# Four units per chunk instead of three and one, and both first weight blocks split before the chunk loop

## The reference

```python
def _ffn_sublayer(h, mod, g_pre, g_post, w_in, w_out):
    shift, scale, gate = mod
    u = _modulate(_rmsnorm(h, g_pre), shift, scale)      # rmsnorm, then * (1 + scale) + shift
    a, b = jnp.split(u @ w_in, 2, axis=-1)
    y = (jax.nn.silu(a) * b) @ w_out
    return h + MACARON_W * gate * _rmsnorm(y, g_post)
```

## Time and profile before

| what | us |
|---|---|
| median of three timed runs | 2501.28 |
| span of the profiled execution | 2505.6 |
| TensorE matmul busy | 2363.2 (94%) |
| VectorE busy | 1239.4 (49%) |
| ScalarE busy | 1023.2 (41%) |
| the two-part products (L914 to L916), share of the chain that ended last | 66% |

### The profile page before, as it was taken

One profiled execution on the slowest core, in us unless ns is written; L12 is line 12 of the kernel. 1 busy time (PEld: TensorE's weight loads), 2 busy tenths in 40 slices (PEclk: granted clock), 3 DMA queues, 4 the chain that ended last, 5 costly groups with the idle time before them and its releaser, 6 DMA issues.

```text
span 2505.6 us, 41414 instructions
## 1 busy us (share of the span) xinstructions
PE 2363.2 (94%) x15342; PEld 2029.3 (81%) x15342; DVE 1239.4 (49%) x1709; ACT 1023.2 (41%) x1459; POOL 33.5 (1%) x35
## 2 busy tenths in 40 slices
PE   5999999999898999998999999899799989998998
PEld 5888888777677888887888878777699979988997
DVE  4332335755656322337332336655564576856665
ACT  4332224543455332235322224543564455344443
POOL 0000000000000000000000000000000000000000
PEclk8999999899998999998999999999899988999899
DMA  9553552322214544532323543421256543214221
GB/s 303 185 176 94 172 177 86 118 85 85 85 35 135 157 141 138 173 124 72 110 79 113 186 140 96 105 89 58 68 148 172 153 143 96 68 61 135 79 68 51
DMA packets 396899, 298.16 MB, mean 119 GB/s; under 512 B 10846, under 2 KB 358756, under 8 KB 396644
## 3 DMA queue, kind: packets, MB, share of 16 engines
q1 hardware_dynamic: 363274, 231.12, 31.3%
q10 hardware_dynamic: 33498, 65.35, 7.4%
HBM read 295.38 MB, written 1.06 MB: 118 GB/s over the span
## 4 chain that ended last, share of the span: by engine, by line
PE 80%; DVE 9%; ACT 4%; issue 3%; DMA 2%; SPq 1%; DVEq 0%; POOL 0%; ACTq 0%; POOLq 0%
PE banks L914 22%; PE banks L915 22%; PE banks L916 22%; PE banks L1172 3%; DVE wl L2095 3%; PE banks L819 2%; ACT wh L1601 2%; PE banks L855 1%; SPq L670 1%; DVE wl L2113 1%; PE banks L1023 1%; ACT uR L1592 1%; DMA scratch<-in_ada_w 1%; PE banks L1044 1%; ACT yT L1593 1%
## 5 line engine op out<-in xcount | busy, mean ns | idle before, releaser
L914 PE MATMUL banks<-uR,wh 128*128 128x512 f32 (+2 forms) x2368 | 837.2, 354 | 41.7 <-DVE uR L2080 25.7
L915 PE MATMUL banks<-uR,wh 128*128 128x512 f32 (+2 forms) x2368 | 822.9, 348 | 0.0
L916 PE MATMUL banks<-uR,wl 128*128 128x512 f32 (+2 forms) x2368 | 821.6, 347 | 0.0
L2095 DVE TENSOR_TENSOR wl<-wraw,wh 128x2048 fp32r<-128x2048 f32 (+2 forms) x214 | 453.1, 2117 | 426.2 <-ACTq L1541 421.4
L1601 ACT ACTIVATE wh<-wraw 128x2048 fp32r<-128x2048 f32 (+2 forms) x224 | 398.7, 1780 | 478.6 <-PE banks L916 448.9
L914 PEld LDWEIGHTS banks<-uR,wh 128*128 128x128 f32 (+1 forms) x2368 | 460.6, 194 | 105.2 <-issue 41.1
L916 PEld LDWEIGHTS banks<-uR,wl 128*128 128x128 f32 (+1 forms) x2368 | 459.9, 194 | 52.9
L915 PEld LDWEIGHTS banks<-uR,wh 128*128 128x128 f32 (+1 forms) x2368 | 460.7, 195 | 49.9 <-issue 0.5
L914 PE MATMUL banks<-gR,wh 128*128 128x512 f32 (+1 forms) x704 | 256.3, 364 | 4.2 <-DVEq L2001 4.1
L915 PE MATMUL banks<-gR,wh 128*128 128x512 f32 (+1 forms) x704 | 255.2, 363 | 0.0
L916 PE MATMUL banks<-gR,wl 128*128 128x512 f32 (+1 forms) x704 | 255.2, 362 | 0.0
(11 more groups left out here) (305 smaller groups left out, 2419.9 us busy)
## 6 DMA issues: line engine op xcount, KB each, us to landing
wraw<-in_ffn_w_in SPq DMA_DIRECT2D x176, 512.0 KB, 5.1
ada_buf<-in_ada_w ACTq DMA_DIRECT2D x27, 2048.0 KB, 8.4
wraw<-in_w_in SPq DMA_DIRECT2D x56, 512.0 KB, 4.6
wraw<-in_ffn_w_out SPq DMA_DIRECT2D x64, 384.0 KB, 4.0
wraw<-in_ffn_w_out SPq DMA_DIRECT2D x64, 320.0 KB, 3.7
wraw<-in_da_w_in SPq DMA_DIRECT2D x24, 512.0 KB, 4.6
wraw<-in_na_w_in SPq DMA_DIRECT2D x24, 512.0 KB, 4.5
yT<-in_ada_w ACTq DMA_DIRECT2D x4, 2048.0 KB, 8.6
```

What stands on the lines that cost most here:

```text
L914: mm(o, a[0], b[0], start=first, stop=False)
L915: mm(o, a[0], b[1], start=False, stop=False)
L916: return mm(o, a[1], b[0], start=False, stop=last)
L2095: do(V.tensor_tensor(wl[:, s, 0:n], wraw[:, s, 0:n], wh[:, s, 0:n].bitcast(F32), ALU.subtract), w_lo)
```

## The change

It does three things at the start of each of the six stages.

1. `together` gets four units: both units of B0 and both of B1. It takes 12 matmuls per chunk, not 9, and no unit runs alone behind the loop. The number of matmuls is the same. The fourth unit needs a fourth bank: in da and na bank 7 instead of 5 (`FIRST_BANKS`), in the FFN stages the fourth of the `gemm` banks.
2. B1 is split whole before the chunk loop. `w_half` is gone; PE waits for `w_lo` of B0 and of B1 before its first matmul of the stage. The splits are in halves by rows of the slot, no longer by columns.
3. In `residual` all halves come one place earlier. Behind an FFN stage the first half of B0 now stands before the first variance, the second behind it, the first half of B1 before the reading of the third sums (L2172 in the kernel before), and its second half behind the second variance. Behind da and na, B0 has been split by then, and the halves of B1 stand behind the first and the second variance.

In ffn00 and ffn01 the transposition of the adaLN row (`ada_turn`, L829) on PE now comes behind the fourth unit. ScalarE's and SyncE's instructions and their order are the same.

```diff
+        FIRST_BANKS = (2, 3, 6, 7)
...
-                    ins = [product_step(o, both(ws[j // 2], k, slice(j % 2 * P, j % 2 * P + P)), (rhs2 if j == 2 and rhs2 else rhs)(k),
+                    ins = [product_step(o, both(ws[j // 2], k, slice(j % 2 * P, j % 2 * P + P)), (rhs2 if j >= 2 and rhs2 else rhs)(k),
...
             def first_weights():
-
-                w = weights(0, DC, 256)
-                pe.wait_ge(w_half, tl["half"].up())
-                return [w, [x[:, 1, 0:DC * 256].rearrange("p (k n) -> p k n", k=DC) for x in (wh, wl)]]
+                return [weights(s, DC, 256) for s in range(2)]
...
-                os = [ga("unit", n) for n in range(-8, -5)]
+                os = [ga("unit", n) for n in range(-8, -4)]
...
-                w = weights(1, DC, 256)
...
-                                for ins in together([gbank()[:, 0:T - c0] for a in range(3)], ws, lambda k: both(u2, k, slice(c0, T)),
+                                for ins in together([gbank()[:, 0:T - c0] for a in range(4)], ws, lambda k: both(u2, k, slice(c0, T)),
                                                     [u0 + len(streams) * (k + 1) for k in range(DC)]):
                                     ins.then_inc(gemm_full, 1)
+                            if first:
                                 continue
                             w = weights(s, DC, 2 * P)
-                            for a in range(1 if first else 0, 2):
+                            for a in range(2):
...
+                b = tl["split"].n
                 early, x, root = stat[:, 0, 8:8 + 3 * nt], stat[:, 0, 20:20 + nt], stat[:, 1, 0:nt]
                 o, free = product(small)
                 do(V.tensor_scalar(early[:, 0:nt], o[:, 0:nt], 1.0 / D, EPS, ALU.mult, ALU.add))
                 do(V.tensor_copy(early[:, nt:3 * nt], o[:, nt:3 * nt]), free)
+                if st.startswith("ffn"):
+                    rest_part(b, 0)
                 o, free = product(small)
                 do(stt(stat[:, 0, 0:nt], o[:, 0:nt], 1.0 / D, early[:, 0:nt], ALU.mult, ALU.add), free, var_ready)
-                b = tl["split"].n
                 if st.startswith("ffn"):
-                    rest_part(b, 0, False)
+                    rest_part(b, 1)
                     b += 1
+                else:
+                    rest_part(b, 0)
                 dve.wait_ge(root_ready, tl["root"].up())
                 two_parts(0, nt)
                 if st.startswith("ffn"):
-                    rest_part(b - 1, 1, False, w_lo)
+                    rest_part(b, 0)
...
-                if to in SUB:
-                    rest_part(b, 0, True, w_half)
-                else:
-                    rest_part(b, 0, False)
-                if to not in SUB or to == "na":
-                    rest_part(b, 1, to in SUB, w_lo)
+                rest_part(b, 1)
...
-                if to in SUB and to != "na":
-                    rest_part(b, 1, True, w_lo)
```

More of the change, by code:

```diff
@@ L328, in build @@
         gy_ready = sem("gy_ready")
-        w_half = sem("w_half")
         gm_ready = sem("gm_ready")
@@ L593, in take @@
                 uses[bank] += 1
-            for n in range(-8, -5):
-                take(("unit", n), 6 if n == -6 else n + 10)
+            for n in range(-8, -4):
+                take(("unit", n), FIRST_BANKS[n + 8])
             for n in DA_STEPS:
                 g, i = da_unit(n)
-                if i is not None and n >= -5:
-                    take(("unit", n), n + 10 if n < -4 else None)
+                if i is not None and n >= -4:
+                    take(("unit", n))
                 if da_rot(n) is not None:
@@ L621, in na_products @@
             for m in range(-8, 24):
-                bank = 6 if m == -6 else m + 10 if m < -4 else turn % 2
+                bank = FIRST_BANKS[m + 8] if m < -4 else turn % 2
                 turn += m >= -4
@@ L806, in _ @@
             tl = {k: Tally() for k in ("u", "g", "w", "sq", "sum", "diag", "qkv", "v", "probn", "probT", "bias", "on",
-                                       "vh", "aa", "ada", "adat", "p", "sq2", "half")}
+                                       "vh", "aa", "ada", "adat", "p", "sq2")}
             mm = nc.tensor.matmul
@@ L985, in da_heads @@
                     if i is not None:
-                        if n >= -5 and i in (0, 2, 4):
+                        if n >= -4 and i in (0, 2, 4):
                             w = weights((3 * g + i // 2) % 2, DC, 256)
-                        if n >= -5:
+                        if n >= -4:
                             o = ga("unit", n)
@@ L1080, in na_heads @@
                 ws = first_weights()
-                os = [unit_bank(m) for m in (-8, -7, -6)]
-                for ins in together([*os[0:2], os[2][:, 0:SEQ]], ws, lambda k: both(u2, k),
+                os = [unit_bank(m) for m in range(-8, -4)]
+                for ins in together([*os[0:2], *[o[:, 0:SEQ] for o in os[2:4]]], ws, lambda k: both(u2, k),
                                     [u0 + 2 * (k + 1) for k in range(DC)], lambda k: both(u2, k, slice(CTX, T))):
                     ins.then_inc(ga_full, 1)
-                w = weights(1, DC, 256)
                 for m in NA_STEPS:
@@ L1089, in na_heads @@
                     n, j = divmod(m, 2)
-                    if i is not None and m >= -5:
+                    if i is not None and m >= -4:
                         if i in (0, 2, 4):
@@ L2100, in rest_next, with rest_part @@
                     rest(b % 2, SIZES[b])
-            def rest_part(b, j, by_columns, *signals):
+            def rest_part(b, j):
                 if b < len(SIZES):
@@ L2109, in half_of @@
                     def half_of(x):
-                        x = x[:, b % 2, 0:2 * n]
-                        return x.rearrange("p (k n) -> p k n", k=DC)[:, :, j * P:j * P + P] if by_columns else x[:, j * n:j * n + n]
-                    do(V.tensor_tensor(half_of(wl), half_of(wraw), half_of(wh).bitcast(F32), ALU.subtract), *signals)
+                        return x[:, b % 2, j * n:j * n + n]
+                    do(V.tensor_tensor(half_of(wl), half_of(wraw), half_of(wh).bitcast(F32), ALU.subtract), *([w_lo] if j else []))
             def residual(st, c0, streams, chunk, to):
@@ L2615, in _ @@
                 rest_next()
-            dve.sem_inc(w_half, 1)
             for n in range(2, ADA_HEAD - 1):
```

## The result

The changed kernel takes 2521.82 us in the median (2519.20 to 2526.46, 4 runs), beside 2499.86 us for the kernel before on the same chip: ratio 1.0090 [1.0076, 1.0103], 22 us slower. The forecast was 2520. The profiled execution after has a time of 2526.46 us, the longest of the four, and a span of 2524.6 us, 19.0 longer than the profiled span before.

The account below looks back on a forecast made before the run. PE, busy for 94% of the span, was taken to bound the kernel. Exposed split 15.9, seam halves 1.4 and clock 2 made +19 us on 2501.3, so 2520 us, with an 8-in-10 range of 2509 to 2528.

Parts of the forecast that it names:

- The fourth unit in the loop: Chunk loops of the six stages: PE waits for no chunks in five, so all four units finish as before; gain 0.
- The exposed split: Behind the four units: B2's split starts 21 matmuls later and PE idles for it in five stages, +15.9 us.
- The rule on double buffering: Skill's advice to overlap loading with compute; both slots now held until the same moment, so B2's split is exposed each start.
- The halves in the seam: DVE's half-splits between stages, moved one place earlier, delay the next loop where idle time does not cover them: +1.4 us.
- The clock: Behind PE's new waits for B2: one fall of the granted clock to half, about +2 us, ends 0 and 8.5.
- the rival of a dearer clock: Every new wait drops PE's clock and later starts lengthen cold heads: +26 us, 2527 us; chance 0.12.
- One of two waits did it: Sign for the dearer clock: of two 2.9 us waits in the earlier trace, one was followed by clock 0.50.
- given back later: Behind B2, ACT or DVE set the pace, so half of 15.9 us is recovered: +9, 2510 us; chance 0.09.
- The loop fills a real gap: In the chunk loops PE does wait for chunks, so the fourth unit is partly free: -11.6, 2490 us; chance 0.05.
- no change: A start keeps its wait for three units (a bank not free), so the time stays 2501 us; chance 0.04.

Follow-up runs that it names:

- Three and one: Changed kernel with three units per chunk in the loop and B1's second unit alone behind it again: 2502.68 us, ratio 1.0009.
- the lag: Changed kernel with all four units in the loop, but B1's two units three chunks behind B0's: 2506.05 us, ratio 1.0028.
- the table load: Changed kernel with a one-column Silu ahead of each FFN stage's loops, moving ACT's 1.28 us table load off B2's chain: 2520.93 us, ratio 1.0081.
- the version that beats both: Kernel before with the one-column Silu and, in na, B2's lead ahead of the evictions and seam halves in the changed order: 2495.21 us, ratio 0.9983.
- the kernel before with the Silu: Kernel before with one Silu of a single column ahead of the FFN stages' loops and nothing else: 2496.68 us, ratio 0.9991.
- the filled waits: Changed kernel with 85 extra 512-column matmuls into an unused bank ahead of the first product with B2: 2516.25 us, ratio 1.0066.
- the run with the lead first: Changed kernel, but in da and na ACT makes B2's high part (lead) before evicting B0's two units: 2527.47 us, ratio 1.0111.
- the repeated one: The changed kernel again with no edit, timed beside the kernel before on one chip: 2522.96 us, ratio 1.0106.

## Why the prediction was right, and where it was not

*The fourth unit in the loop: 0.* Right. The windows over the four units kept their length to 0.4 us in da, ffn10 and ffn11, and in no loop of the changed kernel did PE wait for a chunk after the first.

*The exposed split: +15.9.* Right in mechanism, and in size as a sum. The loops grew by 16.4 us in one profile and 16.1 in the other. The waits came as 4.13, 2.65, 2.69, 3.42, 4.69 and 5.44 where about 4.2, 2.4, 2.4, 3.4, 5 and 5.4 were forecast, and they repeat to 0.06. By stage the loops grew by 2.6, 4.4, 1.9, 3.8, 0.9 and 2.8 us in the first profile (ffn00 to ffn11 in order) and by 4.2, 4.6, 1.3, 2.6, 1.1 and 2.3 in the second, against 2.6, 4.4, 2.8, 3.6, 0 and 2.5. So the good match of the first is in part luck: the clock within the loops moves single stages by up to 1.6 us between executions. Three and one takes the whole of the growth away, the lag most of it, and the table load and the evictions show that pieces of the chain count in full. The rule on double buffering that the prediction weighed (the Trainium skill, Trainium Kernel Development and Optimization, Best Practices) pointed the right way, but it speaks of transfers beside compute and not of when a slot comes free. That is what decided here: with three and one, both slots held the same blocks as early as in the changed kernel, and only the moment at which the first slot came free differed.

In na the forecast was 0, since the loop there went at DVE's pace, and PE's longer wait (4.69 for 2.17) is nearly all the time by which the fourth unit ended earlier. The +0.9 of the profile goes with the clock. In the changed kernel PE has no idle time left in na's loop, so a slower head delays B0's units. The first 18.6 us of the loop lost 2.7 and 2.9 us in the two profiles of the changed kernel ((1 - clock) x time), with loops of 24.15 and 24.36 us; with the table moved it lost 1.6 us and the loop took 23.36, as good as before (23.24).

*The halves in the seam: +1.4.* ffn10's loop starts 1.26 us later in the profiles with no fall behind ffn01's wait (377.7 for 376.44; 1.3 forecast), and na's 0.7 to 0.8 earlier with no fall behind ffn10's (0.7 forecast). To da the forecast was +0.3 and the runs say +1.25: in the two experiments on the kernel before that stretch is 377.23 us, and in five of the seven profiles of the changed one and its variants 378.48 to 378.51. The cover of 1.08 us that the earlier trace rows show there was an accident of that one execution. Windows before (PE alone), and the same instruction of DVE as in the first of the earlier trace rows in the version that beats both:

```profile
436.00:440.00 4.00, 4.00 (x30) 0.75 0.00 0
440.00:444.00 4.00, 4.00 (x21) 0.50 0.00 0
```

```profile
438.78 0.16 DVE L2040 SCALAR_TENSOR_TENSOR stat<-banks,stat 128x4 f32<-128x4 f32 x1 [0.15 <-DVE stat L2166]
```

PE was late there because its clock had fallen. In the version that beats both, and in the kernel before with the Silu, the clock stayed up to that point (1.00 from 434 to 438 us) and DVE has only 0.15 us of idle time, behind its own copy. So the term was about +2.4 and not +1.4, if its parts to ffn11 and hy0, which no run singles out, are as forecast.

*The clock: +2 (0 to 8.5).* This is the step that failed in size, and the rival of a dearer clock had the better number for it. One fall was forecast; five of six waits in either profile are followed by one, and behind the longest ones it can last for two windows. The matmuls behind the waits lost at least 8.5 and 10.1 us in the records, and the filled waits put the net effect at 6 to 9 us. Na's wait, left out as costing nothing, brought the dearest fall in the first profile.

The three FFN stages with a rest in the table, and the same stretches of the run with the lead first, price a fall in time. With a fall behind the wait, the rest is 380.00 and 380.11 us (ffn00), 379.06 and 379.32 (ffn01), 370.01 to 370.03 in three profiles (ffn10); in the variants of the changed kernel without one it is 378.48 to 378.51, 377.67 to 377.71 and 368.30 to 368.45. So one fall costs 1.4 to 1.7 us of the kernel's time, close to the 1.7 that the prediction took from the earlier trace rows. The price was right and the number of falls wrong.

How often a wait for B2 was followed by a fall, over all ten profiles:

| wait of PE for B2, us | waits | with a fall |
|---|---|---|
| 0.3 to 1.7 | 11 | 0 |
| 2.17 to 2.53 | 4 | 1 |
| 2.65 to 2.71 | 6 | 4 |
| 2.92 to 3.42 | 8 | 4 |
| 3.72 to 5.44 | 11 | 11 |

Between 2.17 and 3.42 us it is 9 of 18, and the same wait of 3.42 us went without a fall in one execution and with one in the next. "One of two waits did it" in the earlier trace rows was fair evidence for a half chance each, although the last of these rows ends 0.2 us behind the wait and doesn't show what came after (it was 1.00). With six waits that would have been three falls and 5 us; I took one, and left ffn00, ffn01 and na out.

*The sum.* 15.5 for the waits and the seam and 6 to 9 for the clock make the measured 22 to 24; the forecast had 16 + 1.4 + 2. Taken one by one, the terms of the first profile would add up to more: 16.4 for the loops, 2.4 for the seam and 8.5 for the clock are 27, where hy0's loop starts 21 us later. A part of the difference is the da stage, which was 2.4 us shorter from B2 to the next loop in this profile (293.32 for 295.67) in spite of its fall; in the other profiles it lies between 294.4 and 296.6, with no order by wait or fall. That the forecast came so near is therefore in part luck. The rival "given back later" is refuted: the loops grew by 16.4 us and the start of hy0's loop moved by 21, so nothing was given back in the sum. "The loop fills a real gap" is refuted by the windows over the four units, and "no change" by the result.

## What to carry to other kernels

Before work is pulled forward into a loop, ask what it was covering where it stood. With two slots, the last work that needs only the second slot is the cover for refilling the first; the length of that tail, less the length of the refill chain, is the slack, and it is lost when both slots are released together. And a new wait amid full-clock matmuls is to be priced with its own length and with the clock behind it: in this kernel 1.5 us or more for a wait of 3.7 us or longer, the same half of the time for one of 2.2 to 3.4, and nothing for one of 1.65 or less, even where the trace has a wait of the same length with no fall.

A cover read from one profiled execution may be the trace of an accident: look at the granted clock around it before leaning on it.

## What the runs showed of the hardware

The hybrid stages vary by themselves, in steps. From PE's first matmul with hy0's B2 to hy1's loop it is 216.2 us in the profile before and in three others, 214.5 in the after profile, 212.3 or 212.4 in the repeated one, the one with the lag and the version that beats both, and 210.0 in two (filled waits, and the Silu in the kernel before). Windows over the same stretch of hy1, from 27.4 us behind its first product matmul, PE alone, before and in the version that beats both:

```profile
2300.00:2370.00 70.00, 70.00 (x485) 0.88 0.35 101
```

```profile
2290.84:2360.84 70.00, 70.00 (x525) 0.95 0.35 101
```

The same code gets a clock of 0.88 or 0.95 there, with 485 or 525 matmuls in 70 us: the first in seven profiles, the second in three. From hy1's loop to the end the three take 229.4 us and the seven 232.7 to 233.0. That is some 3 to 6 us per hybrid stage, more than several of the effects above, and why the stage marks were of more use than the spans. What tips it one way or the other, no run here shows.

The ten runs with the lag lie at 2502 to 2503 us (five), at 2509 (one) and at 2512 to 2515 (four). Whether the hybrid stages part them isn't shown, since only one of the ten, at 2502, has a profile.
